# Four slots instead of three for Up's combined tiles, and the reload of h issued by GpSimd

## The reference

```
h = rmsnorm(x, g_pre_mlp[l])
u = jnp.square(jax.nn.relu(jnp.einsum('bsd,df->bsf', h, w_up[l])))     # "Up",   1024 -> 4096
x = x + rmsnorm(jnp.einsum('bsf,fd->bsd', u, w_down[l]), g_post_mlp[l]) # "Down", 4096 -> 1024
```

## Time and profile before

| | |
|---|---|
| median of 3 runs (lowest, highest) | 2818.8 us (2818.32, 2822.24) |
| the profiled execution, its own time | 2821.49 us |
| its span, first to last instruction | 2819.8 us |
| TensorE busy in it | 2735.3 us (97%) |
| VectorE, ScalarE, GpSimd busy | 1755.8, 1345.3, 630.9 us |
| mean granted TensorE clock | 0.995 of full speed |
| Up, from its first product to Down's first | 1573.5 to 2201.5 us |

### The profile page before, as it was taken

One profiled execution on the slowest core, in us unless ns is written; L12 is line 12 of the kernel. 1 busy time (PEld: TensorE's weight loads), 2 busy tenths in 40 slices (PEclk: granted clock), 3 DMA queues, 4 the chain that ended last, 5 costly groups with the idle time before them and its releaser, 6 DMA issues.

```text
span 2819.8 us, 36796 instructions
## 1 busy us (share of the span) xinstructions
PE 2735.3 (97%) x13362; PEld 2258.7 (80%) x13362; DVE 1755.8 (62%) x2495; ACT 1345.3 (48%) x2413; POOL 630.9 (22%) x558
## 2 busy tenths in 40 slices
PE   8999999989999999999999999999999999999998
PEld 6888888877787887877788787788888888888887
DVE  6211111169889899899746776887777544435567
ACT  5121111169788789688523544454444443322233
POOL 5220011035746556557411100000000000000012
PEclk9999999999999999999999999999999999999999
DMA  5443342464424515413347755565445456556566
GB/s 189 132 152 105 105 138 107 142 149 93 112 71 103 126 46 129 113 56 102 105 134 240 252 184 176 200 207 200 146 151 208 172 186 203 185 165 224 198 219 241
DMA packets 287660, 434.49 MB, mean 154 GB/s; under 512 B 19648, under 2 KB 134592, under 8 KB 287488
## 3 DMA queue, kind: packets, MB, share of 16 engines
q1 hardware_dynamic: 241664, 368.41, 42.6%
q10 hardware_dynamic: 45056, 63.05, 6.2%
q0 software_dynamic: 768, 0.79, 0.1%
HBM read 280.27 MB, written 151.91 MB: 153 GB/s over the span
## 4 chain that ended last, share of the span: by engine, by line
PE 62%; DVE 7%; ACT 5%; issue 4%; DMA 2%; POOL 0%; DVEq 0%; ACTq 0%; POOLq 0%; SPq 0%
PE ml_ps L2838 7%; PE ml_ps L2839 7%; PE ml_ps L2837 7%; PE ml_ps L2807 5%; PE ml_ps L2810 5%; PE ml_ps L2809 5%; PE at_ps_t L1486 5%; PE at_ps_s L1462 4%; PE at_ps_s L1468 4%; PE mo_acc L1801 2%; PE mo_acc L1803 2%; PE mo_acc L1802 2%; PE at_ps_o L1501 2%; PE at_ps_o L1502 2%; ACT at_probs L1313 2%
## 5 line engine op out<-in xcount | busy, mean ns | idle before, releaser
L1361 DVE TENSOR_REDUCE at_nmax<-at_ps_s 128x1 f32<-128x1024 f32 (+7 forms) x384 | 346.5, 905 | 40.2 <-PE at_ps_s L1468 38.0
L2807 PE MATMUL ml_ps<-ml_h_hiM,ml_w_hi 128*128 128x512 f32 x896 | 350.5, 391 | 12.5 <-ACT ml_t L2497 10.5
L2810 PE MATMUL ml_ps<-ml_h_hiM,ml_w_lo 128*128 128x512 f32 x896 | 349.3, 390 | 0.0
L2809 PE MATMUL ml_ps<-ml_h_loM,ml_w_hi 128*128 128x512 f32 x896 | 349.2, 390 | 0.0
L2837 PE MATMUL ml_ps<-ml_b_hi,ml_a_hi 128*128 128x512 f32 x896 | 348.5, 389 | 0.0
L2838 PE MATMUL ml_ps<-ml_b_lo,ml_a_hi 128*128 128x512 f32 x896 | 348.5, 389 | 0.0
L2839 PE MATMUL ml_ps<-ml_b_hi,ml_a_lo 128*128 128x512 f32 x896 | 348.5, 389 | 0.0
L598 DVE SCALAR_TENSOR_TENSOR pj_out_sb<-pj_acc,pj_out_sb 128x512 fp32r<-128x512 f32 x96 | 66.3, 691 | 424.1 <-ACT pj_out_sb L534 424.1
L1370 DVE TENSOR_TENSOR at_p_lo<-at_ps_t,at_p_hi 128x512 fp32r<-128x512 f32 x480 | 279.7, 603 | 37.5 <-ACT at_p_hi L1331 34.2
L1331 ACT ACTIVATE at_p_hi<-at_ps_t 128x512 fp32r<-128x512 f32 x480 | 249.0, 534 | 92.3 <-PE at_ps_t L1486 50.4
L2484 POOL TENSOR_SCALAR ml_ss<-ml_ss 128x1 f32<-128x1 f32 x16 | 17.7, 1107 | 1198.7 <-ACT ml_junk L2577 1198.4
(11 more groups left out here) (264 smaller groups left out, 5988.6 us busy)
## 6 DMA issues: line engine op xcount, KB each, us to landing
ml_a_raw<-ua SPq DMA_DIRECT2D x112, 512.0 KB, 4.0
qk<-pj_out_sb ACTq DMA_DIRECT2D x64, 512.0 KB, 2.8
ml_w_raw<-in_w_up_dram SPq DMA_DIRECT2D x64, 512.0 KB, 4.9
ua<-ml_t SPq DMA_DIRECT2D x128, 256.0 KB, 2.6
ml_b_raw<-in_w_down_dram SPq DMA_DIRECT2D x56, 512.0 KB, 5.0
at_q<-qk SPq DMA_DIRECT2D x96, 256.0 KB
at_k<-qk SPq DMA_DIRECT2D x96, 256.0 KB
ua<-ml_x SPq DMA_DIRECT2D x96, 256.0 KB, 2.4
```

Of the source, the lines that this page charges most:

```text
L1361: dve.tensor_reduce(nmax[:, par, sc.a, s, sc.part:sc.part + 1], ps_s[:, sc.g % 2, 0:sc.width], AX.X, ALU.max, negate=True).then_inc(maxed, 1)
L2807: pe.matmul(to, hi, h_hi[m][:, k, :], start=begins and k == 0, stop=False, skip_group_check=not begins)
L2809: pe.matmul(to, hi, h_lo[m][:, k, :], start=False, stop=False, skip_group_check=not begins)
L2810: last = pe.matmul(to, lo, h_hi[m][:, k, :], start=False, stop=k == 3, skip_group_check=not begins)
```

## The change

The ring of combined tiles gets a fourth slot, at `high(126)`; the room for it comes from a DMA scratch of 8192 bytes, half of what it was. The slots are dealt out by `n % 4`; the first stage of pieces (sweep 0) still counts on three of the semaphores, so `FIRST_STAGE` becomes a list with 0 for the fourth. The stores of `t21` and `t12` share one semaphore ("both"), since a fourth `x_stored` is needed. The waits and the DMA issues of the reload move from SyncE's loop to GpSimd, which issues each group when the sum it waits for has been made.

```diff
-    r.sb("high", [P, 126 * 256])
+    r.sb("high", [P, 128 * 256])
...
-    x_at = low(4), low(6), high(124)
+    x_at = low(4), low(6), high(124), high(126)
...
-    u_stored = {q: r.sem(f"u_stored{q}") for q in ("21", "12", "22", "11")}
-    x_stored = [r.sem(f"x_stored{s}") for s in range(3)]
+    u_stored = {q: r.sem(f"u_stored{q}") for q in ("22", "11", "both")}
+    U_STORES = {"22": 2, "11": 2, "both": 4}
+    x_stored = [r.sem(f"x_stored{s}") for s in range(4)]
...
-    FIRST_STAGE = 16 * 2 * len(pieces) // 3
+    FIRST_STAGE = [16 * 2 * len(pieces) // 3] * 3 + [0]
...
+    def after_turns(eng, slot, turn):
+
+        if FIRST_STAGE[slot] + turn:
+            eng.wait_ge(x_stored[slot], FIRST_STAGE[slot] + 16 * turn)
...
-    x_use = {one: (n % 3, n // 3) for n, one in enumerate(uses)}
+    x_use = {one: (n % 4, n // 4) for n, one in enumerate(uses)}
...
-            if n == 1:
-                sp.wait_ge(h_lo_ready, h_lo_no[0, "M5"])
-                sp.wait_ge(mix.h_stored, 16 * (RT // 2))
-                reload_rows(0)
...
-            if 1 <= n < 5:
-                sp.wait_ge(h_summed, h_sum_no[1, pieces[2 * n - 2]])
-                reload_rows(n)
...
     def _(pool):
         mix.gpsimd(pool)
+        pool.wait_ge(h_lo_ready, h_lo_no[0, "M5"])
+        pool.wait_ge(mix.h_stored, 16 * (RT // 2))
+        for n, group in enumerate(RELOADS):
+            if n:
+                pool.wait_ge(h_summed, h_sum_no[1, pieces[2 * n - 2]])
+            for k in group:
+                pool.dma_start(h_rows[:, k, :], hT[k]).then_inc(h_loaded, 16)
...
             if n:
-                act.wait_ge(u_stored[q], 32 * n)
+                act.wait_ge(u_stored["both"], 64 * n)
...
-    nc = _bacc.Bacc("TRN2", target_bir_lowering=False, num_devices=1)
+    nc = _bacc.Bacc("TRN2", target_bir_lowering=False, num_devices=1, dynamic_dma_scratch_size=8192)
```

More of the change, by code:

```diff
@@ L1968, in wait_staged @@
         for s in range(3):
-            eng.wait_ge(x_stored[s], FIRST_STAGE)
+            eng.wait_ge(x_stored[s], FIRST_STAGE[s])
+    def after_turns(eng, slot, turn):
+        if FIRST_STAGE[slot] + turn:
+            eng.wait_ge(x_stored[slot], FIRST_STAGE[slot] + 16 * turn)
     def sum_piece(dve, sweep, n):
@@ L1981, in sum_piece @@
             to = x_ring[slot]
-            dve.wait_ge(x_stored[slot], FIRST_STAGE + 16 * turn)
+            after_turns(dve, slot, turn)
         dve.tensor_tensor(to[:, :], h_quarter(one)[:, k, :], h_quarter(two)[:, k, :], op).then_inc(h_summed, 1)
@@ L1991, in hi_piece @@
             of, to = x_ring[x_use["piece", n, "sum"][0]], x_split[slot]
-            act.wait_ge(x_stored[slot], FIRST_STAGE + 16 * turn)
+            after_turns(act, slot, turn)
         act.activation(to[:, :], of[:, :], ACT.Copy).then_inc(h_hi_ready, 1)
@@ L2047, in fetch_h @@
             sp.wait_ge(done, 2 * (7 * (UC - 1) + NO[m] + 1))
-            for slot in range(3):
-                sp.wait_ge(x_stored[slot], FIRST_STAGE + 16 * staged_turns[slot])
+            for slot in range(4):
+                after_turns(sp, slot, staged_turns[slot])
         else:
@@ L2169, in mlp @@
             uses += [(n,) + one for one in X_EARLY]
-    x_use = {one: (n % 3, n // 3) for n, one in enumerate(uses)}
+    x_use = {one: (n % 4, n // 4) for n, one in enumerate(uses)}
     last_staged = max(n for n, one in enumerate(uses) if one[0] == "piece")
-    staged_turns = [(last_staged - slot) // 3 + 1 for slot in range(3)]
+    staged_turns = [(last_staged - slot) // 4 + 1 for slot in range(4)]
     def x_tile(n, m, p):
@@ L2390, in store_late @@
                 sp.wait_ge(c_step, c_no(n, "M5", p))
-                sp.dma_start(u_rows(n, "M5", p), t21[p][:, :]).then_inc(u_stored["21"], 16)
+                sp.dma_start(u_rows(n, "M5", p), t21[p][:, :]).then_inc(u_stored["both"], 16)
                 sp.wait_ge(c_step, c_no(n, "M6", p))
-                sp.dma_start(u_rows(n, "M6", p), t12[p][:, :]).then_inc(u_stored["12"], 16)
+                sp.dma_start(u_rows(n, "M6", p), t12[p][:, :]).then_inc(u_stored["both"], 16)
         def wait_stored(n):
             for q in u_stored:
-                sp.wait_ge(u_stored[q], 32 * (n + 1))
+                sp.wait_ge(u_stored[q], 16 * U_STORES[q] * (n + 1))
             last = uses.index((n,) + X_LATE[-1])
[L2399 to L2404, removed]
+            for s in range(4):
+                after_turns(sp, s, (last - s) // 4 + 1)
         for n in range(UN):
-            if n == 1:
-                sp.wait_ge(h_lo_ready, h_lo_no[0, "M5"])
-                sp.wait_ge(mix.h_stored, 16 * (RT // 2))
-                reload_rows(0)
             if n:
@@ L2586, in _ @@
                 for q in u_stored:
-                    act.wait_ge(u_stored[q], 32 * UN)
+                    act.wait_ge(u_stored[q], 16 * U_STORES[q] * UN)
             for i, h, t in ended(step):
@@ L2662, in combine @@
                 to = x_tile(n, m, p)
-                dve.wait_ge(x_sem(n, m, p), FIRST_STAGE + 16 * x_use[n, m, p][1])
+                after_turns(dve, *x_use[n, m, p])
             dve.tensor_tensor(to[:, :], TILES[one][p][:, :], TILES[two][p][:, :], op).then_inc(c_step, 1)
```

## The result

The changed kernel takes 2802.81 us (median of 6 runs, 2801.58 to 2807.93), the kernel before, on the same chip, 2818.56 (6 runs, 2817.20 to 2822.24). The ratio is 0.9944, 95% interval 0.9931 to 0.9957: 15.75 us less, where 13.0 were forecast. The six waits that the forecast is about are gone, at their forecast price. What comes on top is 2.1 us that the sum didn't have, all in Up, and a difference between executions that isn't the change's.

The account below looks back on a forecast made before the run. TensorE was taken to fill nearly all the span, so only its waits in Up count: 10.5 + 0.9 + 1.6 = 13.0 us, costs taken as 0, from 2818.8 to 2805.8 us; range 2803 to 2814.

Parts of the forecast that it names:

- The six waits: Up, first product of M4, sub-blocks 1 to 6: TensorE's waits for `take_m2` vanish, 10.5 us idle plus 0.9 us.
- The clock: Up, behind the longest wait: eight products at 0.43 us instead of 0.23, from TensorE's lower clock; 1.6 us gained.
- So about 2.0 us of lateness in VectorE is free: Up: VectorE can be about 2.0 us late unnoticed; TensorE pays for lateness above that almost one to one.
- The fourth slot and the residue: (M7, 1) stops waiting for its slot; (M1, 0) now wants the same store, leaving 0 to 0.8 us, taken as 0.
- The raw weights: Up: the earlier reload makes them 0 to 3.0 us later, taken as 1.4; covered by the free time, cost 0.
- rival B: Raw weights become the wait: 2808.8 or 2814.8 us, chance 0.15; sign: line 2101 waiting over 3.5 us, sub-blocks 1 to 3.
- GpSimd's transfers: Reload issued from GpSimd in Up: may land slower than SyncE's, but rows are first read 29 us later; cost 0.
- Sub-blocks 7 to 15 gain nothing, as their waits are under the free 2.0.: Up, sub-blocks 7 to 15: VectorE's waits for stores stay under the 2.0 us of free lateness, so 0 gained.
- A term that was too small: Up: each of TensorE's six waits costs 0.15 us more than its idle time, 0.9 us in all.
- the medians' own spread: Whole kernel: 1 us of variation between medians, allowed for in the forecast's own range of 2803 to 2809.

Follow-up runs that it names:

- small-edits kernel: Kernel before with only the smaller DMA scratch and the shared semaphore for stores of t21 and t12; three slots, reload by SyncE: 2821.01 us, ratio 1.0005.
- reordered kernel: Kernel before, three slots, with SyncE issuing the reload behind the early stores instead of ahead of them: 2805.77 us, ratio 0.9958.
- second set: Repeat runs of two kernels against the kernel before: the whole change 2805.79 us, ratio 0.9950; the fourth slot alone, reload by SyncE, 2804.91 us, ratio 0.9952.
- SyncE's early reload: Fourth slot alone, but SyncE issues the reload early, right ahead of the raw weights: 2806.56 us, ratio 0.9954 to the kernel before.
- doubled reload: Changed kernel with GpSimd copying each group from the second on once more, to a spare DRAM tensor: 2809.43 us, ratio 0.9968 to the kernel before.

## Where the prediction was right, and which step failed

**The six waits: right.** 11.4 us were forecast for them, 11.5 were lost in the profile before and none after. The small-edits kernel has them, the slot alone has none.

**The clock: right.** 1.6 forecast, 1.6 measured, though by seven products at 0.43 us and two at 0.33 where the prediction counted eight at 0.43. The granted clock is 1.00 all through Up after.

**"So about 2.0 us of lateness in VectorE is free": right as an average.** It holds in the slot alone (2.70 late, 0.68 waited), in GpSimd's reload alone (3.2 late in two parts, 1.24 waited) and in the reordered kernel (2.45 late, 0.3 waited). From place to place it isn't a constant: where (M7, 1) alone is late, the profiles of kernels with three slots show 1.1 to 2.4 us free. The least is at the end of sub-block 0, where 1.50 us of waiting gave TensorE 0.20 us in before and 0.43 with the small edits; the prediction took the 0.20 into its sum and left this pair out of its rule.

**The fourth slot and the residue: right in kind.** (M1, 0) waits 1.01 us in the profile after ("under 1 us" was forecast) and up to 2.70 with SyncE's reload in front; TensorE's wait is 0 with the move, 0 to 0.7 without it.

**The raw weights: right.** 1.4 us later were forecast, 1.2 to 1.9 measured in sub-blocks 1 to 3 of both profiles. The row in sub-block 3, 3.58 us, is over the 3.5 us that the prediction set as the sign of rival B, and B didn't come: the sign counted the 1.7 us that were waited there before, and what matters is the lateness that is new.

**GpSimd's transfers: right to take 0.** 7.1 us to landing against a cover of 29. The prediction took a rule of the Trainium skill, page "SBUF — State Buffer", section "SBUF: two separate sides", as speaking against this. It doesn't: the rule has GpSimd locked out while VectorE runs an operation in a 2-port mode, and the same page says under "Who interferes with whom" that `tensor_tensor` has no such mode. All that VectorE runs between these issues and their landing is `tensor_tensor`. The trace agrees that nothing is held up. The window of after from the issue at 1710.18 on (length, VectorE busy and instructions, granted clock, share of the DMA engines, GB/s):

```profile
1710.00:1719.00 9.00, 6.07 (x7) 1.00 1.01 336
```

VectorE is busy for two thirds of it, the DMA engines are full, and the transfers land as SyncE's do in the same place (7.1 and 6.9 us). No run here shows the lock at work. The other page cited from the Trainium skill, "DMA: Bandwidth & Descriptors", section "Issuing engines are not separate DMA queues", has transfers of all issuing engines interleave on the same 16 DMA engines. The traces agree: whichever engine issues the 1.05 MB, the raw weights of sub-blocks 1 to 3 are late by the same 1 to 2 us.

**The step that failed: "Sub-blocks 7 to 15 gain nothing, as their waits are under the free 2.0."** They gain 1.25 us, all in sub-block 8: 0.30 at M4, where (M7, 1) had waited 1.88 us and 0.14 us of idle time went unseen, and 0.94 at M3. There are two ways from a late VectorE to TensorE, and the sum followed one of them, by `take_m2` to M4. The other goes on in VectorE's own order. The timeline of VectorE before, sub-blocks 7 to 8:

```profile
1896.83 0.69 DVE L2664 TENSOR_TENSOR ml_x<-ml_t,ml_t 128x512 f32<-128x512 f32 x1 [1.88 <-DMA ua<-ml_x]
...
1902.78 1.21 DVE L2127 TENSOR_TENSOR ml_w_lo<-ml_w_raw,ml_w_hi 128x1024 fp32r<-128x1024 f32 x1
...
1905.05 3.48 DVE L2036 TENSOR_TENSOR ml_h_loM<-mo_h_rows,ml_h_hiM 128x1024 fp32r<-128x1024 f32 x3
```

and that of TensorE:

```profile
1907.51 0.47 PE L2807 MATMUL ml_ps<-ml_h_hiM,ml_w_hi 128*128 128x512 f32 x1 [0.78 <-issue]
```

The product is the first of M3. In this sub-block, the first of the second half of the rows, VectorE makes new low halves of `h`: three operations from 1905.05, of which the first two (to 1907.40) are M3's. Line 2800 of the kernel makes TensorE wait for them, and it starts at 1907.51, 0.11 us behind the second. VectorE had lost 1.88 us at (M7, 1), and VectorE does not idle between that place and these operations, so the lateness arrives here whole. This path has little cover: after, the second low half ends 0.45 us ahead of M3's start, so about 0.3 us would be free (an estimate, 0.45 less 0.11). The wait stands in the profile as "issue", so a count of waits by the name `take_m2` passes over it. After, no wait for a store stands ahead of the three low halves:

```profile
1887.01 3.50 DVE L2042 TENSOR_TENSOR ml_h_loM<-mo_h_rows,ml_h_hiM 128x1024 fp32r<-128x1024 f32 x3
```

and TensorE runs through M3. Some 0.9 us at this place are lost in all kernels with three slots (before 0.94; GpSimd's reload alone, the small edits and the reordered one 0.92, 0.92, 0.91). With four slots nothing is lost in five of the six profiles, and 0.19 us in the second one of the slot alone, where the raw weights of sub-block 7 had been waited for 1.97 us. In each profile that loses time here, M3 starts 0.10 or 0.11 us behind the second low half, and in the others later than that. So the low halves release this product, and the three slots make them late.

**A term that was too small.** A wait was priced at its idle time and 0.15 us. The products behind a restart start about 0.1 us further apart than usual in sum, eight times: 0.85 us.

With these two, 1.25 + 0.85 = 2.1 us, the 13.0 become 15.1, and Up shows 15.1. By the forecast's own base, 2818.8, they give 2803.7, which is inside the range: they use up most of its lower part, and the rest, down to 2802.81, is no effect of the change. The prediction gave the medians' own spread 1 us. Six runs of the same changed kernel in the second set have a median 3.0 us higher, 12.1 us below before instead of 15.75, and all twelve together, 2804.2, would have lain inside the range. So the mechanism and most of the price were right, 2.1 us were missing from the sum, the spread was put too small, and the side of 2803 on which the median fell was chance.

**What the parts are worth.** Against the one profile of before: the fourth slot alone 13.9 to 15.3 us of Up; GpSimd's move alone 9.4; SyncE's order alone 13.5; both parts 15.1. Against the profile of the small edits each is 1.9 less. They are ways to the same gain, not summands. The move of the reload costs 1 to 2 us of raw-weight lateness, which is hidden beside the fourth slot, and brings at most 1.2 us there. Whether the change is faster than the slot alone can't be told from the medians (2804.2 and 2805.4).

## What to carry to other kernels

Before a buffer is added for a store that lands late, look at what stands in the queue ahead of that store: three moved lines took 13.5 us off Up here, where the whole change took 15.1, and the medians of the two in one set of runs are equal. When the free time of an engine is found from one waiting reader, look for its other readers, above all in the one sub-block whose work differs from the rest, and count waits named "issue" with the others. Lateness from two causes on one engine is added before it is set against the free time; while the sum stays under it, both cost nothing.

## What the runs showed that was not expected

TensorE's granted clock falls in attention in some executions and not in others, with the same work ahead. The windows at 620 us (length, PE busy and products, granted clock, share of the DMA engines, GB/s), before:

```profile
620.00:622.00 2.00, 0.51 (x1) 0.78 0.00 0
622.00:624.00 2.00, 2.00 (x6) 0.50 0.35 131
```

and in the kernel with the reordered queue, which is the same up to Up:

```profile
620.00:622.00 2.00, 0.72 (x3) 1.00 0.00 0
622.00:624.00 2.00, 2.00 (x16) 1.00 0.35 131
```

Both were idle for 2.22 us. In one the next products run at the lower level (1.2 GHz, 0.50), six in 2 us, in the other at the full 2.4, sixteen. The same comes near 930 and 1130 us, about 1.5 us each time and 4.3 us for the three, the difference in attention (814.1 and 809.7 us). The profiles of before, of GpSimd's reload alone, of the small edits and of SyncE's early reload have all three dips; those of after, of the slot alone (both), of the doubled reload and of the reordered queue have none; the second one of the changed kernel has the one at 1130 and one near 1331. Another dip comes near 22 us, in the input projection, in the profiles of after, of the small edits and the second of the slot alone, and Up's start shows its 1.6 us. So the dips belong to neither slots, scratch nor engine of the reload. What decides them is open. Those in attention are almost a third of the gain studied here, and they are probably why one kernel's runs lie near 2802 and near 2806, and why medians of six of them differ by 3 us. The mean granted clock of every run bears this out: of the changed kernel's twelve runs, the six up to 2803.6 us have 0.997 or 0.998, the six from 2804.8 us on 0.995 or 0.996. Where in the run it fell is seen only in the profiled executions.
